# Odd mixer of a two-block kernel: the norm's root behind the projections, gate weights and compressed keys as the standing operand

## Reference

```python
def second_block(x, ...):                      # x: 512 tokens x 1024
    for layer in range(2):
        h = rms_norm_2(x, ln_mix_pre[layer])   # x * rsqrt(mean(x*x) + eps) * g
        m = even_mixer(h, ...) if layer == 0 else odd_mixer(h, ...)
        x = x + rms_norm_2(m, ln_mix_post[layer])
        h = rms_norm_2(x, ln_ffn_pre[layer])
        x = x + rms_norm_2(swiglu(h, ...), ln_ffn_post[layer])
...
def odd_mixer(h, ...):
    z = h @ w_in
    q, kc, vc, ks, vs, kw, vw, gt, rq, rk, rv, rg = split(z)
    y_c = nsa_attention(q, kc, vc, ks, vs, kw, vw, gt, ...)
    y_d = retention(rq, rk, rv, rg, ...)
    return concatenate([y_c, y_d]) @ w_out
```

## Time and profile before

| | us |
|---|---|
| median of three executions | 3647.01 (3642.53 to 3650.95) |
| profiled execution | 3645.06 |
| its span in the trace | 3643.3 |
| mean granted TensorE clock | 0.965 of 2.4 GHz |
| TensorE, VectorE, ScalarE, GpSimd busy | 3397.2, 1958.3, 1390.5, 337.2 |

### The profile page before, as it was taken

One profiled execution on the slowest core, in us unless ns is written; L12 is line 12 of the kernel. 1 busy time (PEld: TensorE's weight loads), 2 busy tenths in 40 slices (PEclk: granted clock), 3 DMA queues, 4 the chain that ended last, 5 costly groups with the idle time before them and its releaser, 6 DMA issues.

```text
span 3643.3 us, 42168 instructions
## 1 busy us (share of the span) xinstructions
PE 3397.2 (93%) x17474; PEld 2853.0 (78%) x17474; DVE 1958.3 (54%) x2786; ACT 1390.5 (38%) x2191; POOL 337.2 (9%) x278
## 2 busy tenths in 40 slices
PE   7889898999999998899899999899999889989997
PEld 6778777888888886787677888777888677768886
DVE  5674655667736635856545645546343456344343
ACT  4563434234313324644434324344222346243221
POOL 0010000221101110000011101220000210210002
PEclk9998999999999999999899999999999889999999
DMA  5101114343323421011233322322222111112322
GB/s 210 35 23 61 45 43 151 136 149 121 112 89 120 138 88 51 20 62 50 75 131 119 124 101 88 107 93 84 90 101 98 72 47 36 47 58 97 106 86 71
DMA packets 74495, 321.94 MB, mean 88 GB/s; under 512 B 8896, under 2 KB 17856, under 8 KB 52288
## 3 DMA queue, kind: packets, MB, share of 16 engines
q1 hardware_dynamic: 74304, 319.25, 25.5%
HBM read 303.49 MB, written 15.73 MB: 88 GB/s over the span
## 4 chain that ended last, share of the span: by engine, by line
PE 50%; DVE 4%; ACT 4%; issue 1%; POOL 1%; DMA 0%; POOLq 0%; ACTq 0%; DVEq 0%; SPq 0%
PE psum L660 14%; PE psum L662 14%; PE psum L661 14%; PE psum L1171 1%; ACT split_weights L620 1%; DVE split_weights L631 1%; PE psum L1203 1%; POOL arena L2058 1%; ACT arena L1317 0%; PE psum L2816 0%; PE psum L673 0%; PE psum L2472 0%; DVE arena L1494 0%; PE psum L675 0%; PE psum L674 0%
## 5 line engine op out<-in xcount | busy, mean ns | idle before, releaser
L660 PE MATMUL psum<-split_inputs,split_weights 128*128 128x512 f32 (+1 forms) x2872 | 1057.0, 368 | 16.3 <-DVE split_weights L631 10.1
L661 PE MATMUL psum<-split_inputs,split_weights 128*128 128x512 f32 (+1 forms) x2872 | 1048.6, 365 | 0.0
L662 PE MATMUL psum<-split_inputs,split_weights 128*128 128x512 f32 (+1 forms) x2872 | 1047.0, 365 | 0.0
L631 DVE TENSOR_TENSOR split_weights<-arena,split_weights 128x2048 fp32r<-128x2048 f32 (+3 forms) x246 | 507.5, 2063 | 479.1 <-ACT split_weights L620 478.8
L660 PEld LDWEIGHTS psum<-split_inputs,split_weights 128*128 128x128 f32 x2872 | 546.8, 190 | 109.9 <-DVE split_weights L631 13.2
L661 PEld LDWEIGHTS psum<-split_inputs,split_weights 128*128 128x128 f32 x2872 | 546.1, 190 | 87.1 <-issue 2.9
L662 PEld LDWEIGHTS psum<-split_inputs,split_weights 128*128 128x128 f32 x2872 | 545.7, 190 | 86.7
L620 ACT ACTIVATE split_weights<-arena 128x2048 fp32r<-128x2048 f32 (+3 forms) x246 | 414.0, 1683 | 163.6 <-PE psum L662 163.5
L660 PE MATMUL psum<-split_hidden,split_weights 128*128 128x512 f32 (+1 forms) x880 | 324.1, 368 | 1.7 <-DVE split_weights L631 1.6
L661 PE MATMUL psum<-split_hidden,split_weights 128*128 128x512 f32 (+1 forms) x880 | 323.9, 368 | 0.0
L662 PE MATMUL psum<-split_hidden,split_weights 128*128 128x512 f32 (+1 forms) x880 | 323.7, 368 | 0.0
(11 more groups left out here) (335 smaller groups left out, 4940.3 us busy)
## 6 DMA issues: line engine op xcount, KB each, us to landing
arena<-w_up_dram SPq DMA_DIRECT2D x44, 1024.0 KB, 5.0
arena<-ffn_up_dram SPq DMA_DIRECT2D x44, 1024.0 KB, 4.8
arena<-w_ada_dram SPq DMA_DIRECT2D x80, 512.0 KB, 3.7
arena<-w_in_dram SPq DMA_DIRECT2D x32, 1024.0 KB, 4.8
arena<-w_down_dram SPq DMA_DIRECT2D x32, 704.0 KB, 4.1
arena<-ffn_down_dram SPq DMA_DIRECT2D x32, 704.0 KB, 4.1
arena<-od_w_in_dram SPq DMA_DIRECT2D x13, 1024.0 KB, 4.7
arena<-w_ada_dram SPq DMA_DIRECT2D x8, 1024.0 KB, 12.8
```

Of the source, the lines that this page charges most:

```text
L631: dve.e.tensor_tensor(ws[:, i, 1, 0:nk * w], raw_view(key), ws[:, i, 0, 0:nk * w].bitcast(F32), ALU.subtract).then_inc(*w_lo(*key))
L660: pe.e.matmul(dst, a[0], b[0], start=i == 0, stop=False)
L661: pe.e.matmul(dst, a[0], b[1], start=False, stop=False)
L662: ins = pe.e.matmul(dst, a[1], b[0], start=False, stop=i == n - 1)
```

## The change

- Seam of layer 0's FFN to the odd mixer: written like the other seam. DVE scales, adds (L2031, L2035 in the new numbers) and takes low parts (L1995), ScalarE the high parts; `pool_post_norm`, `dve_pre_norm` and the squares ahead of the projection are gone there. Each engine that splits weights prepares one more block ahead of the seam.
- The squares for the odd mixer are formed behind that, six of the additions on GpSimd, and summed on TensorE behind the projections of kc, vc, ks and kw. The root multiplies vc (DVE), the rotary tables `sinn`, `cosn` and those of retention `sinr`, `cosr` (DVE), and, as four columns `r_col` made by DVE with a product by the identity and a sum (L2553), the evictions of values, gates and rv. rg is multiplied on DVE by a copy of the root, `r_kept`, ahead of its silu.
- Gates: the 24 weight columns stand and 512 tokens stream, in one bank; behind q0 four transposes (L2496) turn the rows, and the sigmoid reads them.
- Compressed scores: the keys stand, padded with zeros to 128 columns so that four heads share a bank; 512 queries stream (L2741, 16 matmuls). ScalarE copies the rows out, eight transposes (L2747) turn them. GpSimd clears the pads.
- Fillers of the attention are left out of slots that score the last query tile, and so reach to later slots.
- The load of the compression's second weights waits for the sum of squares instead of vc.

```diff
+        def act_gained_highs(site, l, gname, y_site):
             for c in range(DC):
                 act.wait_ge(halves_sum, y_site, c)
-                act.e.activation(h2_part(c, *ALL)[0], X2[:, c, :], ACT.Copy, scale=v2(l, "ffn_pre", c)).then_inc(
+                act.e.activation(h2_part(c, *ALL)[0], X2[:, c, :], ACT.Copy, scale=v2(l, gname, c)).then_inc(
                     *h_hi(site, c))
             for c in range(DC):
                 act_square_summed(site, ALL, c, DC, T2, 1, X2[:, c, :])
...
-        def dve_pre_norm(site, l, gname):
-            y_of = first_y if site == "mix_0" else pre_y
+        def dve_first_norm(site):
+            y_of = first_y
             dve.wait_ge(rooted, site, ALL)
             for c in range(DC + 1):
                 if c < DC:
                     y = y_of.take(dve, site, c)
-                    x, gain_c, r = X2[:, c, :], v2(l, gname, c), rstd[:, 0, :]
-                    if site == "mix_0":
-                        x, gain_c, r = X1[:, c, LAT[0]:LAT[1]], both_gain[:, c:c + 1], rstd[:, 1, :]
+                    x, gain_c, r = X1[:, c, LAT[0]:LAT[1]], both_gain[:, c:c + 1], rstd[:, 1, :]
...
-        def dve_post_gained(site, l, then):
+        def dve_post_gained(site, l, gname, then, then_l, then_gname):
             dve.wait_ge(rooted, site, ALL)
             for c in range(DC + 2):
                 if c < DC:
-                    dve.e.scalar_tensor_tensor(out=MX[:, c, :], in0=MX[:, c, :], scalar=v2(l, "mix_post", c),
+                    dve.e.scalar_tensor_tensor(out=MX[:, c, :], in0=MX[:, c, :], scalar=v2(l, gname, c),
                                                in1=rstd[:, 0, :], op0=ALU.mult, op1=ALU.mult).then_inc(*normed(site, c))
                 if 0 < c <= DC:
                     dve.wait_ge(normed, site, c - 1)
                     dve.e.tensor_tensor(X2[:, c - 1, :], X2[:, c - 1, :], MX[:, c - 1, :], ALU.add).then_inc(
                         *halves_sum(site, c - 1))
                 if c > 1:
-                    dve_gained(then, l, c - 2)
+                    dve_gained(then, v2(then_l, then_gname, c - 2), c - 2)
...
+            if l == 0:
+                act_prepare()
...
-        KCK, KCL = od2(2, 32, words=split_words), od2(2, 32, words=split_words)
...
+        r_col, r_junk = od2(TT), od2(P)
+        r_kept = sinn
...
+        key_words = NPT[1].rearrange("p s t -> p (s t)")[:, 0:4 * 224]
+        padded_keys = key_words.rearrange("p (g y n) -> p g y n", g=2, y=2)
+        KCK, KCL = (padded_keys[:, :, y, 96:128] for y in range(2))
+        cmp_rows = (KX, KY)
...
+        def pe_gates():
+            w = pe_block("od_w_in", 0, 3)
+            ps = banks.take(pe, "od", "gt", place=turn6.next())
+            mm3(ps[0:24, :], [(w(k, 0, 24), h2_part(k, *ALL)) for k in range(DC)]).then_inc(*product("od", "gt"))
+
+        def pe_gates_turn():
+            ps = banks.take(pe, "gt_turn", place=turn6.next())
+            pe.wait_ge(copied, "od", "gt")
+            for tt in range(TT):
+                ins = pe.e.transpose(ps[:, tt * 24:(tt + 1) * 24], gate_rows[:, tt * P:(tt + 1) * P], ident[0:24, 0:24])
+            ins.then_inc(*turned("gt"))
+
+        def act_gates():
+            act.wait_ge(product, "od", "gt")
+            act.e.activation(gate_rows, banks.at("od", "gt")[0:24, :], ACT.Copy).then_inc(
+                *banks.back(("od", "gt"), copied, "od", "gt"))
+
+        def act_gates_turn():
+            act.wait_ge(turned, "gt")
+            src = banks.at("gt_turn")[:, 0:TT * 24]
+            for tt in range(TT):
+                ins = act.e.activation(GT[:, tt, :], src[:, tt * 24:(tt + 1) * 24], ACT.Sigmoid, scale=r_col[:, tt:tt + 1])
+            ins.then_inc(*banks.back(("gt_turn",), activated, "gt"))
+
+        def pe_odd_keys(site):
+            gates = pre_gates(site)
+            pe_side([("od", "kc"), ("od", "vc")], pe_block("od_w_in", 0, 0), gates)
+            pe_ends(("od_w_in", 0, 0), "od", "vc")
+            w = pe_block("od_w_in", 0, 1)
+            for j, what in enumerate(("ks", "kw")):
+                pe_project(("od", what), w, j * P, h2_part, DC, gates)
+            pe_ends(("od_w_in", 0, 1), "od", "kw")
+            pe_square_summed(site, ALL, DC, T2, 1)
+            pe_tokens(("od", "v"), pe_block("od_w_in", 0, 2), 256, gates)
+            pe_ends(("od_w_in", 0, 2), "od", "v", TT - 1)
+            for what, view in KEYS_ROPED:
+                pe_rope2(what, view)
+            pe_gates()
+            pe_ends(("od_w_in", 0, 3), "od", "gt")
+
+        def act_odd_keys(site):
+            act_evict(("od", "kc"), KC)
+            act_prepare()
+            act_evict(("od", "ks"), KX)
+            act_evict(("od", "kw"), KY)
+            act_log(site, ALL, DC, T2, 1, D)
+            act_root(site, ALL, T2, 1)
+            act_tables(SIGMOID)
+            act_prepare()
+            for tt in range(TT):
+                act.wait_ge(product, "od", "v", tt)
+                act.wait_ge(scaled, "r_col", tt)
+                act.e.activation(NV[:, tt, :, 0:64], token_halves(tt), ACT.Copy, scale=r_col[:, tt:tt + 1]).then_inc(
+                    *w_half("v", tt))
+            act_prepare()
+            act_gates()
+
+        def dve_odd_keys(site):
+            r = rstd[:, 1, :]
+            dve.wait_ge(rooted, site, ALL)
+            dve.wait_ge(product, "od", "vc")
+            dve.e.tensor_tensor(VC, banks.at("od", "vc"), r, ALU.mult).then_inc(
+                *banks.back(("od", "vc"), scaled, "od", "vc"))
+            for tt in range(TT):
+                if tt:
+                    dve.wait_ge(scaled, "r_col", tt - 1)
+                dve.e.tensor_tensor_reduce(r_junk, r[:, tt * P:(tt + 1) * P], ident, 1.0, 0.0, ALU.mult, ALU.add,
+                                           r_col[:, tt:tt + 1]).then_inc(*scaled("r_col", tt))
+            dve.wait_ge(activated, "rotary", 3)
+            for name, table in (("sinn", sinn), ("cosn", cosn)):
+                dve.e.tensor_tensor(table, table, r, ALU.mult).then_inc(*scaled(name))
+            dve_prepare()
+            for tt in range(TT):
+                dve.wait_ge(w_half, "v", tt)
+                dve.wait_ge(scaled, "r_col", tt)
+                dve.e.scalar_tensor_tensor(out=NV[:, tt, :, 64:P], in0=token_halves(tt), scalar=r_col[:, tt:tt + 1],
+                                           in1=NV[:, tt, :, 0:64].bitcast(F32), op0=ALU.mult, op1=ALU.subtract).then_inc(
+                    *banks.back(("od", "v", tt), taken, "nsa_v", tt))
+            dve.wait_ge(scaled, "sinn")
+            for what, _ in KEYS_ROPED:
+                dve_rope2(what)
+            dve_prepare()
+            for name, table in (("sinr", sinr), ("cosr", cosr)):
+                dve.e.tensor_tensor(table, table, r, ALU.mult).then_inc(*scaled(name))
+
+        def pool_odd_keys(site):
+            pool.wait_ge(scaled, "cosn")
+            for n, (what, view) in enumerate(KEYS_ROPED):
+                pool_rope2(what, view)
+                if n == 0:
+                    pool.wait_ge(product, "square", site, ALL, DC - 1)
+                    pool.e.memset(row_all[:, 256:576], 0.0).then_inc(*filled("blocks"))
...
+                    act_evict(("od", f"rv{i}", tt), RV[:, tt, 256 * i:256 * i + 256], ACT.Copy, slice(0, 256),
+                              scale=r_col[:, tt:tt + 1])
...
+            act.wait_ge(filled, "cmp_keys")
...
+            pe.wait_ge(taken, "nsa_k", 1, 1, 1)
+            for b in range(2):
+                ps = banks.take(pe, "cmp_rows", b, place=4 + b)
+                for x in range(4):
+                    h = 4 * b + x
+                    pe.wait_ge(taken, "nsa_q", h)
+                    for y in range(2):
+                        keys = padded_keys[:, h // 4, y, 96 - 32 * x:224 - 32 * x]
+                        ins = pe.e.matmul(ps, keys, QS[:, h, :], start=x + y == 0, stop=x + y == 4)
+                ins.then_inc(*product("cmp_rows", b))
             for b in range(2):
                 ps = banks.take(pe, "cmp_s", b, place=4 + b)
-                for x, (h, qt) in enumerate((h, qt) for h in range(4 * b, 4 * b + 4) for qt in range(TT)):
-                    pe.wait_ge(taken, "nsa_q", h)
-                    q = slice(qt * P, (qt + 1) * P)
-                    s = ps[:, 32 * x:32 * x + 32]
-                    pe.e.matmul(s, QS[:, h, q], KCK[:, h // 4, :], start=True, stop=False)
-                    ins = pe.e.matmul(s, QS[:, h, q], KCL[:, h // 4, :], start=False, stop=True)
+                pe.wait_ge(copied, "cmp_rows", b)
+                for qt in range(TT):
+                    ins = pe.e.transpose(ps[:, qt * P:(qt + 1) * P], cmp_rows[b][:, qt * P:(qt + 1) * P], ident)
                 ins.then_inc(*product("cmp_s", b))
+
+        def act_cmp_rows():
+            for b in range(2):
+                act_evict(("cmp_rows", b), cmp_rows[b])
...
-                            late=late, evict=evict, fill=[pieces.pop(0)] if pieces else [])
```

(26 more changed lines are left out.)

100 lines of the change are left out of this document (37 added, 63 removed).

## The result

The changed kernel takes 3612.16 us (median of four executions, 3608.33 to 3617.56) where the kernel before, run beside it, takes 3647.4 (3642.53 to 3650.95). The ratio is 0.9907, with a 95% interval of 0.9895 to 0.9918: 35 us faster. Its profiled execution took 3611.44 us with a span of 3609.5.

What follows compares the result with a forecast made beforehand. TensorE, busy 93% of the span, was taken as the bound, so gains come from its idle time, slow clock or oversized matmuls. The terms summed to -29.3, giving 3617.7 us against the median 3647.01, range 3603 to 3633.

Steps and rivals of the forecast that it cites:

- rival (1): Attention's tail heals wholly, no stall in slot 36, clock high, no slow stretch behind two waits: about 3608; chance 0.17.
- Seam: From layer 0's FFN to the odd mixer: shrinks from 35.7 to the other seam's 21.8 us, -13.9.
- squares: In the key stretch: the sum of squares comes in behind the projections, two products of about 1 us each, +1.9.
- rival (2): Root not hidden: squares, sums, root and columns hold TensorE in value or rotary products; 3624 to 3630, chance 0.14.
- The term of retention: Retention's four gate evictions become a DVE product plus the same activation; only the last counts: +0.5, 0 to 0.7.
- Gates: Gate projection: 96 matmuls of 24 columns, 16.8 us, become 24 of 512 columns, 5.5 us at full clock: -11.3.
- Compressed scores: 16 matmuls for 64; everything behind hangs on DVE: -5.0, between -3.5 and -6.5; slow clock after TensorE's idling +1.0.
- The third query chunk: Behind the gates, TensorE waits some 2.9 us for weights DVE splits last: +0.5, then +1.0 for slow clock.
- That chain does not get shorter: Queries: from ScalarE's first key split to TensorE's start, 14.8 us before; it starts about 0.5 us later against gates' end.
- Attention: Moved fillers help the tail: -4, between -12 and +5; the -3.0 includes +1.0 for slow clock after the compressed scores.
- Each of the four weight splits follows its filler to another slot and can stall there as before (about 3 us each).: Attention, counted against the gain: stalls moved, not removed; the last split lands in slot 36, 3 us and slow end.
- Rival (3): Slower: filler-less slot pairs let the clock fall, most of attention's 147 us at 1.2 GHz; example 3659, chance 0.03.

Runs made afterwards that it cites:

- before_fill: The kernel before, with one part of the change alone: fillers left out of slots that score the last query tile; 3639.63 us, ratio 0.998.
- gates_back: The changed kernel with the gates alone as before: tokens stand, 24 weight columns stream, 96 matmuls, four evictions; 3624.79 us, ratio 0.9943.
- cmp_back: The changed kernel with the compressed scores alone as before: queries stand, 32 key columns stream, 64 matmuls; 3619.51 us, ratio 0.9926.
- seam_split: The changed kernel with the extra weight split ahead of the seam moved behind the norm's work on ScalarE and DVE; 3629.26 us, ratio 0.9949.
- first_split: The changed kernel with the attention's first weight split moved from ahead of the first row maxima to slot -1's late work; 3611.26 us, ratio 0.9907.
- after: The changed kernel itself, as profiled with the whole change; median 3612.16 us, profiled execution 3611.44 us.
- tables_late: The changed kernel with DVE's two products for retention's rotary tables moved behind the splits of compressed keys and values; 3613.9 us, ratio 0.9916.
- keys_first: As tables_late, and besides ks and kw rotated ahead of kc, and ScalarE evicting the gates behind its key splits; 3612.29 us, ratio 0.9907.
- last_split: The changed kernel with the attention's last weight split moved from slot 36 behind its last slot; 3606.47 us, ratio 0.9901.
- combined: The changed kernel with the edits of keys_first, last_split and first_split together; 3600.82 us, ratio 0.9887.

## Why the prediction was right, and where not

The time lay in the stated range, on the fast side of 3617.7, between the forecast and rival (1). Rival (1) isn't what happened, though: the stall in slot 36 is there, and what went were the three stalls ahead of it. Of the 5.7 us by which the profiles' gain passes the forecast, the attention alone gave 9.1 (-12.1 against -3.0), and the queries and the retention took 3.5 back. That the total is so near is in part luck, as the last point below shows.

- **Seam, squares, retention: right in mechanism and size.** The other seam was the right model, down to its wait (8.02 us against 8.0) and its length (21.80 and 21.8). Squares cost 1.31 us of TensorE, not 1.9. GpSimd's sums, the root and the columns held nobody; rival (2) doesn't occur. The term of retention was +0.5; in the runs in which it began at full clock it is 130.1 against 129.58.
- **Gates: right.** 24 matmuls in 5.95 us at full clock, predicted 5.5, and the old form's cost came back when undone.
- **Compressed scores: right in sum.** -4.81 (-5.0), and 16 matmuls and their eviction up to the first transpose took 6.1 us, predicted 5.9. The weight split ahead of the first row maximum was named as one link of the chain behind the scores; that it alone bounds the wait was not seen, and moving it took the wait away.
- **The third query chunk: mis-sized, +2.1 instead of +0.5.** The step was "That chain does not get shorter". It got longer, from 14.8 to 16.5 us (2887.49 to 2903.96); the later start, +0.4, was forecast as +0.5. The three rotations now come in a row, late, so GpSimd works beside DVE's key splits and copies and both slow each other: 0.8 us on the splits from first to last (7.04 against 6.25), 0.9 on the copies; ks itself lands 0.4 us ahead of ScalarE's first split. The wait was 4.66 us where 2.9 was forecast. Its slow clock, +1.3, was forecast as +1.0.
- **Attention: the step that failed.** "Each of the four weight splits follows its filler to another slot and can stall there as before (about 3 us each)." They did move, and stalled in none of the places but the last: three stalls of 3.17, 2.92 and 3.24 us, with the slow clock behind them, went and did not come back elsewhere. Eight fillers to ten slots bring the splits into step with the work. That much could be read from the order of slots; that the step they now fall on leaves room for a split is what the runs show. The last split did land in slot 36 and stalled for 3.48 us with slow clock behind it, as forecast. That slow clock reached into retention (+1.57 of its +2.11).
- **Rival (3) is real in small.** In ten profiles with the new rule for the fillers whole, five had half clock behind each of the four empty pairs of slots (before_fill, gates_back, cmp_back, seam_split, first_split), three had it behind none (after, tables_late, keys_first), two behind one (last_split, combined). So in eight of ten all four had the same outcome. The price is 1.6 us each, not a whole round at half clock. With four falls the profile of after would have shown some 5 us less gain over attention and retention together (266.56 there against 271.3 in gates_back and cmp_back), about the sum that was forecast: the forecast would have been met by two errors that cancel, the stalls that went and the falls that came.

What decides whether such a wait is followed by half clock stays open. It isn't the instructions, which are the same, nor the length of the wait, 1.27 us in all, and last_split shows both outcomes in one execution. No run here took the wait itself away without moving the splits.
